# A hybrid decoder step on one core: new order of work in both token mixers, with sample numerators and decay logits cut into pieces between dense products

## The chip, the core and the metric

The kernel runs on one core of a Trainium2 chip. The metric is the device time of one execution in microseconds, lower is better. Five engines share the work: TensorE (matrix products, PE in the rows, its weight loads PEld), VectorE (DVE), ScalarE (ACT), GpSimd (POOL, idle here) and SyncE (SP), which issues the transfers.

## What is computed

Two layers, each of FFN, token mixer, FFN, around a residual stream of 576 tokens (8 sample sequences of 8 tokens, one prompt of 512) by 1024 features, in float32:

```python
for l in range(DEPTH):                     # DEPTH = 2
    x = x + 0.5 * swiglu(rmsnorm(x, norm_w[l, 0]), ...)
    h = rmsnorm(x, norm_w[l, 1])
    y = mlstm_mixer(h, ...) if l % 2 == 0 else gla_mixer(h, ...)
    x = x + y
    x = x + 0.5 * swiglu(rmsnorm(x, norm_w[l, 2]), ...)
```

The first mixer (mLSTM) projects to queries and keys (4 heads of 128 each), passes them through a causal convolution over 4 tokens and SiLU, projects values (4 heads of 256), an output gate and two scalar gates per head, and runs a stabilised matrix memory. Prompt tokens are done in chunks of 128, sample tokens against a stored state of 8 x 128 x 256 per head, which is updated and written back. The second mixer (gated linear attention) has no convolution, but a decay for every key feature; the attention inside a chunk is built from eight level products (distances 1, 2, 4, ... 64), and after each level queries, keys and decays are rescaled before the next. Outputs are the token results and all new states.

## The kernel before

Everything is laid out with features on partitions, 576 tokens along the free axis. Each dense weight block (128 x 1024) is loaded into `raw` (4 slots), ScalarE copies it to `w_hi` in the reduced format (L990) and VectorE subtracts to get `w_lo` (`split`, L1310); a dense product is then three passes, high by high, high by low, low by high (`split_product`, 288 columns each, L423; value tiles are 256 columns wide, L613). A pair is two such blocks; `lo_done` tells TensorE that a block's halves are there, `pe_done` that a pair is done, `psum_free` that VectorE has emptied its banks. The order on every engine is written out by hand; each engine takes its instructions in that order, and a wait holds up all that stands behind it.

Around the change:

- **Projection of queries and keys, first mixer** (`mlstm_qk`). Four pairs; pair 0 and 1 give queries, pair 2 and 3 keys. For each pair VectorE runs `split_next`, evacuates the pair into `conv_buf` (`before_conv`), and does three taps for each block (`taps`, L1472); ScalarE does the first tap and SiLU. The gate logits of all heads (`row_logits`, `row_sums`, `row_maxima`, 4 partitions wide) stand behind the taps.
- **Heads, first mixer** (`mlstm_mix`). Per head: five value tiles, two output-gate blocks in halves (`o_part`), and between them scores, transposed keys, updates of the state, the prompt numerator, the sample numerator (`sample_numerator`: 32 products of 8 columns in the trace and 4 of 64, L641 and L644, then the denominators), sums of squares (L675, L677) and sample state updates (L667).
- **Projection and heads, second mixer** (`gla_qk`, `gla_mix`). The decay logits (`decay_logits`, L530) are products with 16 rows. In the head loop level products of head h+2 (L504, L507) stand between the parts of head h. Before a level product TensorE waits on `lq_ready`, which VectorE raises at the end of `take_level` for the level before (L1769 to L1781). VectorE evacuates the sample numerator in `take_sample` (L1577), the prompt's in `take_prompt` (L1585), sample updates in `take_sample_updates` (L1595), the sums in `variance` (L1800, L1801).

The head loop of the second mixer on TensorE before:

```python
o_part(ph, h + 1, 0, 1)
sample_out(h, 4), level(h + 2, at + 1)
o_part(ph, h + 1, 1, 0)
sample_updates_of(h, 0, 4), level(h + 2, at + 2)
o_part(ph, h + 1, 1, 1)
```

and on VectorE, before and after the change:

```python
take_sample(1, h, 4), take_level(h + 2, at + 1)
take_sample_updates(1, h, 0, 4), take_level(h + 2, at + 2)
take_o(ph, h + 1, 1)
take_sample_updates(1, h, 1, 4), take_level(h + 2, at + 3)
```

## Time and profile before

| | |
|---|---|
| median of 3 runs | 2420.64 us (2414.5 to 2421.11) |
| profiled execution, its own time | 2422.03 us |
| its span, first to last instruction | 2420.2 us |
| TensorE busy | 2366.1 us (98%), 17380 products |
| VectorE busy | 1073.6 us (44%) |
| ScalarE busy | 665.7 us (28%) |
| mean granted clock of TensorE | 0.982 |
| transfers | 201.28 MB, mean 83 GB/s |

The chain of waits runs over TensorE for 94% of the span. The clock is given as a share of 2.4 GHz. Where busy time is told for a stretch, an instruction that reaches beyond it counts with its part inside. A product's own duration in the timeline contains its way through the array, so products overlap; their pace is read from the distance of their starts.

### The profile page before, as it was taken

How to read it: one execution, taken by the hardware profiler on the slowest of the kernel's cores; microseconds unless marked ns; L12 is line 12 of the kernel's file. 1: busy time of each engine (PE TensorE's matmuls, PEld its weight loads, DVE VectorE, ACT ScalarE, POOL GpSimd, SP SyncE). 2: the span in 40 equal slices, each digit the busy share in tenths (PEclk: the TensorE clock that was granted, in tenths of full speed). 3: DMA queues.
4: the chain of work that ended last, by engine and by line, in shares of the span. 5: the costliest groups of instructions: out<-in, count | busy, mean ns of one | idle time of the engine just before them, and what ended most of it. 6: DMA issues, size and time to landing. Idle time of an engine off the chain costs nothing.

```text
span 2420.2 us, 39582 instructions
## 1 busy us (share of the span) xinstructions
PE 2366.1 (98%) x17380; PEld 2332.7 (96%) x17380; DVE 1073.6 (44%) x1378; ACT 665.7 (28%) x801; POOL 0.2 (0%) x4
## 2 busy tenths in 40 slices
PE   7999999889999999999999999999999999999996
PEld 7999999889999999999999999999999899999996
DVE  5434324575445443334554333353764444334234
ACT  4212213443233321222332122234221333212122
POOL 0000000000000000000000000000000000000000
PEclk9999999999989999999999999999999999999998
DMA  4222222133222222222222222222122222222221
GB/s 169 87 87 70 86 87 70 60 106 104 87 77 92 87 87 70 87 87 66 91 87 84 73 87 87 65 91 88 50 76 73 86 76 87 87 87 74 83 74 52
DMA packets 71399, 201.28 MB, mean 83 GB/s; under 512 B 7140, under 2 KB 24804, under 8 KB 71296
## 3 DMA queue, kind: packets, MB, share of 16 engines
q1 hardware_dynamic: 71296, 199.79, 25.5%
q8 instruction: 78, 1.28, 0.2%
q14 instruction: 25, 0.20, 0.0%
HBM read 187.82 MB, written 11.95 MB: 83 GB/s over the span
## 4 chain that ended last, share of the span: by engine, by line
PE 94%; DVE 3%; ACT 1%; issue 1%; DMA 1%; SPq 0%; DVEq 0%; ACTq 0%
PE ps L423 82%; PE ps L613 4%; PE ps L504 1%; PE ps L641 1%; PE ps L667 1%; PE ps L475 1%; DVE scratch L1472 1%; PE ps L675 1%; PE ps L630 1%; PE ps L656 1%; DVE w_lo L1310 1%; PE ps L659 0%; DMA bc<-rows_all 0%; ACT w_hi L990 0%; DVE scratch L1339 0%
## 5 line engine op out<-in xcount | busy, mean ns | idle before, releaser
L423 PE MATMUL ps<-xn_hi,w_hi 128*128 128x288 f32 x3328 | 722.0, 299 | 23.1 <-DVE w_lo L1310 20.0
L423 PE MATMUL ps<-xn_hi,w_lo 128*128 128x288 f32 x3328 | 715.8, 297 | 0.0
L423 PE MATMUL ps<-xn_lo,w_hi 128*128 128x288 f32 x3328 | 715.7, 297 | 0.0
L423 PEld LDWEIGHTS ps<-xn_hi,w_hi 128*128 128x128 f32 x3328 | 540.2, 190 | 26.7 <-DVE w_lo L1310 12.1
L423 PEld LDWEIGHTS ps<-xn_lo,w_hi 128*128 128x128 f32 x3328 | 539.9, 190 | 0.0
L423 PEld LDWEIGHTS ps<-xn_hi,w_lo 128*128 128x128 f32 x3328 | 539.3, 190 | 0.0
L990 ACT ACTIVATE w_hi<-raw 128x1024 fp32r<-128x1024 f32 x336 | 335.4, 1046 | 360.7 <-PE ps L423 330.1
L1310 DVE TENSOR_TENSOR w_lo<-raw,w_hi 128x1024 fp32r<-128x1024 f32 x336 | 395.9, 1219 | 62.2 <-ACT w_hi L990 60.1
L423 PE MATMUL ps<-h_lo,w_hi 128*128 128x288 f32 x1664 | 358.5, 297 | 2.6 <-DVE h_hi L1610 2.6
L423 PE MATMUL ps<-h_hi,w_hi 128*128 128x288 f32 x1664 | 358.0, 297 | 0.0
L1348 DVE TENSOR_TENSOR scratch<-ps,rstd 128x576 f32<-128x576 f32 x88 | 66.6, 757 | 536.9 <-PE ps L423 533.9
L423 PE MATMUL ps<-h_hi,w_lo 128*128 128x288 f32 x1408 | 301.4, 296 | 0.0
L423 PEld LDWEIGHTS ps<-h_lo,w_hi 128*128 128x128 f32 x1664 | 269.5, 190 | 3.4 <-DVE h_hi L1610 3.4
L423 PEld LDWEIGHTS ps<-h_hi,w_hi 128*128 128x128 f32 x1664 | 269.4, 190 | 0.7 <-DVE h_lo L1357 0.7
L1022 ACT ACTIVATE scratch<-scratch 128x576 f32<-128x576 f32 x88 | 60.4, 687 | 723.2 <-DVE scratch L1348 723.1
L1379 DVE SCALAR_TENSOR_TENSOR x<-ps,x 128x1152 f32<-128x1152 f32 x56 | 76.0, 1357 | 353.9 <-PE ps L423 353.9
L423 PEld LDWEIGHTS ps<-h_hi,w_lo 128*128 128x128 f32 x1408 | 226.9, 189 | 0.0
L613 PE MATMUL ps<-w_hi,xn_hi 128*128 128x256 f32 x320 | 98.3, 307 | 3.8 <-DVE w_lo L1310 3.8
L1357 DVE TENSOR_TENSOR h_lo<-scratch,h_hi 128x576 fp32r<-128x576 f32 (+1 forms) x88 | 66.8, 759 | 73.8 <-ACT h_hi L1024 73.8
L613 PE MATMUL ps<-w_hi,xn_lo 128*128 128x256 f32 x320 | 94.8, 296 | 0.0
L613 PE MATMUL ps<-w_lo,xn_hi 128*128 128x256 f32 x320 | 94.6, 296 | 0.0
L1024 ACT ACTIVATE h_hi<-scratch 128x576 fp32r<-128x576 f32 (+1 forms) x88 | 60.4, 686 | 81.2 <-DVE scratch L1354 81.2
(209 smaller groups left out, 1507.8 us busy)
## 6 DMA issues: line engine op xcount, KB each, us to landing
raw<-in_w_gate SPq DMA_DIRECT2D x88, 512.0 KB, 3.7
raw<-in_w_up SPq DMA_DIRECT2D x88, 512.0 KB, 4.5
raw<-in_w_down SPq DMA_DIRECT2D x64, 512.0 KB, 3.9
raw<-in_w_mix SPq DMA_DIRECT2D x64, 512.0 KB, 4.1
raw<-in_w_down SPq DMA_DIRECT2D x32, 384.0 KB, 3.5
state_s<-in_state_c SPq DMA_DIRECT2D x4, 1024.0 KB, 8.1
out_c_s<-state_s SPq DMA_DIRECT2D x4, 1024.0 KB, 4.5
state_s<-in_state_g SPq DMA_DIRECT2D x4, 1024.0 KB, 7.6
```

The costliest lines, as they stand in the source:

```text
L423: ins = nc.tensor.matmul(o, a, b[:, c] if c is not None else b, start=first and j == 0, stop=last and j == 2)
L475: ins = nc.tensor.matmul(ps[:, j, HALF_TOK:HALF_TOK + 192], ones, T2(5)[:, a, 192 * j:192 * (j + 1)], start=a == 0, stop=a == 1)
L504: ins = nc.tensor.matmul(ps[:, bank, c * P:(c + 1) * P], left[:, ts], right[:, ts], start=True, stop=True)
L613: ins = nc.tensor.matmul(out, a[:, k, xs], b[:, 2 * half:2 * half + 2, ws], start=k == 0 and j == 0, stop=k == KT_X - 1 and j == 2)
L630: ins = nc.tensor.matmul(ps[:, 4 + c // 2, (c % 2) * DV:(c % 2 + 1) * DV], k_tok[:, c, :], v_tok[:, 1 + c, h * DV:(h + 1) * DV], start=Tru ...
L990: nc.scalar.activation(w_hi[:, slot, :], raw[:, slot, :], ACT.Copy).then_inc(hi_done, 1)
L1022: nc.scalar.activation(T(0), T(0), ACT.Silu).then_inc(silu_done, 1)
L1024: nc.scalar.activation(h_hi[:, bass.ds(m, 1), :].rearrange("p o t -> p (o t)"), T(2), ACT.Copy)\
L1310: V.tensor_tensor(w_lo[:, slot, :], raw[:, slot, :], w_hi[:, slot, :].bitcast(f32), ALU.subtract).then_inc(lo_done, 1)
L1348: V.tensor_tensor(cut2(T(0)), ps[:, b:b + 2, 0:HALF_TOK], cut2(rstd[:, :]), ALU.mult)\
L1357: V.tensor_tensor(h_lo[:, bass.ds(m, 1), :].rearrange("p o t -> p (o t)"), T(2), hh, ALU.subtract)\
L1379: ins = V.scalar_tensor_tensor(xs, ps[:, b:b + 4, 0:HALF_TOK], scale, xs, ALU.mult, ALU.add)
```

## The change

1. First mixer, projection: the queries and keys of one head form a pair (the weight blocks are laid out in that order). The split of the pair after next stands ahead of the convolution work on VectorE and ScalarE; `conv_buf` has four buffers in place of two; the tap results lie in `og` in three places; half of the taps are moved into the head stage. Rows for the broadcast are transferred ahead of one weight load.
2. First mixer, heads: TensorE, VectorE and ScalarE get a new order; gate columns come after the first value tile, sums of squares later, and for head 1 also updates and keys.
3. Sample numerators of both mixers run in pieces (`sample_piece`), each behind the products of one k of a dense block: eight pieces in a value tile, four in half a gate block.
4. Second mixer: decay logits are issued one head at a time inside the second block of a pair; the parts of head h move one place later on TensorE, relative to the level products. `gla_mix` of VectorE and ScalarE is as before.
5. Keys are signalled (`ktok_ready`) before the batch copies are made (`ktb_ready`).

```diff
-                load_mix(base + 2, 0, 10)
                 sp.wait_ge(rexp_done, 1)
                 for row, src in enumerate((T(6), T(7), T(3))):
                     sp.dma_start(io["rows"][row, :, :], src[0:N_HEADS, :]).then_inc(rows_out, 16)
-                load_mix(base + 3, 0, 18)
+                load_mix(base + 2, 0, 10)
                 sp.wait_ge(rows_out, 48)
-                sp.wait_ge(silu_qk, KT_X)
-                sp.wait_ge(tail_done, KT_X)
                 rows_load(0, bc_m, 0)
                 rows_load(1, bc_w, 0)
                 rows_load(2, bc_f, 0)
+                load_mix(base + 3, 0, 18)
+                sp.wait_ge(conv_ready, KT_X)
...
+            def sample_piece(mixer, h, bank, i, n):
+
+                a, per = 2 * i // n, 2 * DEC_BATCH // n
+                vs = slice(h * DV + a * P, h * DV + (a + 1) * P)
+                ds = slice(a * P, (a + 1) * P)
+                first = (i % (n // 2)) * per
+                for b in range(first, first + per):
+                    ts = slice(b * DEC_SEQ, (b + 1) * DEC_SEQ)
+                    nc.tensor.matmul(ps[:, bank, a * SAMPLE + b * DEC_SEQ:a * SAMPLE + (b + 1) * DEC_SEQ],
+                                     state_s[:, b, ds], qt[:, h, ts],
+                                     start=b == 0, stop=True, skip_group_check=True)
+                if first + per == DEC_BATCH:
+                    ins = nc.tensor.matmul(ps[:, bank, a * SAMPLE:(a + 1) * SAMPLE], v_tok[0:SAMPLE, 0, vs],
+                                           att(mixer, h)[0:SAMPLE, SEQ:TOK], start=False, stop=True,
+                                           skip_group_check=True)
+                    if a == 1 and mixer == 1:
+                        ins.then_inc(num_s_done, 1)
...
+                            if mixer == 1 and pp == 2 and blk == 1 and k in (0, 4):
+                                if k == 0:
+                                    pe.wait_ge(psum_free, base + 2)
+                                    pe.wait_ge(alow_ready, 1)
+                                decay_logits(k // 4, 4 + k // 2)
+                            if mixer == 1 and pp == 3 and blk == 1 and k in (0, 4):
+                                if k == 0:
+                                    pe.wait_ge(psum_free, base + 3)
+                                decay_logits(2 + k // 4, k // 2)
                         if blk == 0 and pp == 0:
                             early_gates(mixer, base)
-                        if mixer == 1 and blk == 0 and pp == 2:
-                            pe.wait_ge(psum_free, base + 2)
-                            pe.wait_ge(alow_ready, 1)
-                            decay_logits(0, 4)
-                            decay_logits(1, 6)
-                        if mixer == 1 and blk == 0 and pp == 3:
-                            pe.wait_ge(psum_free, base + 3)
-                            decay_logits(2, 0)
-                            decay_logits(3, 2)
...
                 for h in range(N_HEADS):
                     if h == 0:
                         rstd_columns(ph)
                     v_tile(ph, h, 0)
-                    v_tile(ph, h, 1)
-                    if h:
-                        sums_of(h - 1), scores(h)
+                    if h == 0:
+                        gate_columns()
+                    if h == 1:
+                        v_tile(ph, h, 1, sample_part(0))
+                        sample_den(0)
+                    else:
+                        v_tile(ph, h, 1)
+                    if h > 1:
+                        sums_of(h - 1)
+                    if h != 1:
+                        scores(h)
                     v_tile(ph, h, 2)
-                    if h:
+                    if h == 1:
+                        sums_of(0), scores(1)
+                    if h > 1:
                         sample_updates_of(h - 1, 0)
-                    else:
-                        gate_columns()
                     v_tile(ph, h, 3)
                     if h:
-                        sample_updates_of(h - 1, 1)
+                        sample_updates_of(h - 1, 0 if h == 1 else 1)
+                    v_tile(ph, h, 4)
+                    if h == 1:
+                        sample_updates_of(0, 1)
+                    if h != 1:
+                        keys_out(h)
+                    o_part(ph, h, 0, 0)
+                    if h == 1:
+                        keys_out(1)
                     else:
-                        scores(0)
-                    v_tile(ph, h, 4)
-                    keys_out(h)
-                    o_part(ph, h, 0, 0)
-                    updates_of(h)
+                        updates_of(h)
                     o_part(ph, h, 0, 1)
+                    if h == 1:
+                        updates_of(1)
                     o_part(ph, h, 1, 0)
                     prompt_out(h)
-                    o_part(ph, h, 1, 1)
-                    sample_out(h)
+                    if h:
+                        o_part(ph, h, 1, 1, sample_part(h))
+                        sample_den(h)
+                    else:
+                        o_part(ph, h, 1, 1)
...
                     updates_of(h), level(h + 2, at)
                     o_part(ph, h + 1, 0, 1)
-                    sample_out(h, 4), level(h + 2, at + 1)
-                    o_part(ph, h + 1, 1, 0)
-                    sample_updates_of(h, 0, 4), level(h + 2, at + 2)
+                    level(h + 2, at + 1)
+                    o_part(ph, h + 1, 1, 0, sample_part(h, 4))
+                    level(h + 2, at + 2)
                     o_part(ph, h + 1, 1, 1)
-                    sample_updates_of(h, 1, 4), level(h + 2, at + 3)
+                    sample_updates_of(h, 0, 4), level(h + 2, at + 3)
                     v_tile(ph, h + 1, 0)
-                    prompt_out(h), level(h + 2, at + 4)
+                    sample_updates_of(h, 1, 4), level(h + 2, at + 4)
                     v_tile(ph, h + 1, 1)
-                    sums_of(h, 4), level(h + 2, at + 5)
+                    prompt_out(h), level(h + 2, at + 5)
                     v_tile(ph, h + 1, 2)
+                    sums_of(h, 4)
                     if h == 0:
                         level(2, 7)
                         v_tile(ph, 1, 3)
...
                         v_tile(ph, 1, 4)
                         level(3, 1)
                     else:
+                        v_tile(ph, 2, 3)
                         keys_out(2)
-                        v_tile(ph, 2, 3)
...
+                R, base = slice(0, N_HEADS), ph["base"]
+                first_tap, silu = mlstm_conv(base)
+                split(ph, 0, 1)
+                gates_copy(0)
+                split(ph, 1, 0)
+                norm_root(ph["norm"])
+                first_tap(0)
+                first_tap(1)
+                act.wait_ge(rz_ready, 1)
+                own(nc.scalar.activation(T(5)[R], T(5)[R], ACT.Exp))
+                nc.scalar.activation(T(5)[R], T(5)[R], ACT.Ln, bias=1.0).then_inc(rz_exp, 1)
+                silu(0)
+                split(ph, 1, 1)
+                first_tap(2)
+                act.wait_ge(rexp_ready, 1)
+                nc.scalar.activation(T(5)[R], T(5)[R], ACT.Exp)
+                nc.scalar.activation(T(7)[R], T(7)[R], ACT.Exp)
+                nc.scalar.activation(T(3)[R], T(3)[R], ACT.Exp).then_inc(rexp_done, 1)
+                silu(1)
+                first_tap(3)
+                split(PHASES[j + 1], 0, 0)
+                silu(2)
+                first_tap(4)
+                silu(3)
+                first_tap(5)
+                split(PHASES[j + 1], 0, 1)
...
+                base = ph["base"]
+                split(ph, 0, 1)
+                dve.wait_ge(pe_done, base + 1)
+                norm_variance()
+                split(ph, 1, 0)
+                dve.wait_ge(rstd_ready, ph["norm"] + 1)
+                V.memset(conv_buf[:, :, CONV_P:CONV_P + TAIL], 0.0)
+                before_conv(0)
+                before_conv(1)
+                row_logits()
+                taps(0)
+                row_sums()
+                dve.wait_ge(pe_done, base + 2)
+                before_conv(2)
+                before_conv(3)
+                split(ph, 1, 1)
+                row_maxima()
+                taps(1)
+                dve.wait_ge(pe_done, base + 3)
+                before_conv(4)
+                before_conv(5)
+                split(PHASES[j + 1], 0, 0)
+                taps(2)
+                taps(3)
+                dve.wait_ge(pe_done, base + 4)
+                before_conv(6)
+                before_conv(7)
+                split(PHASES[j + 1], 0, 1)
...
+                take_rstd(0)
+                take_columns()
+                exponents(0)
+                taps(4)
+                take_v(ph, 0, 0)
+                take_scores(0)
+                taps(5)
+                take_v(ph, 0, 1)
+                taps(6)
+                take_v(ph, 0, 2)
+                take_keys(0)
+                taps(7)
+                split_at(2)
+                take_updates(0)
+                take_o(ph, 0, 0)
+                exponents(1)
+                for h in range(1, N_HEADS):
+                    take_o(ph, h - 1, 1)
+                    take_prompt(0, h - 1)
+                    if h == 1:
+                        split_at(3)
+                        take_v(ph, 1, 0)
+                    take_sample(0, h - 1, 7)
+                    denominator(h - 1)
+                    if h > 1:
+                        split_at(2 * h + 1)
                         take_v(ph, h, 0)
-                        variance(h - 1)
-                        take_scores(h)
-                        take_sample_updates(0, h - 1, 0, 4)
-                        take_v(ph, h, 1)
+                    variance(h - 1)
+                    take_scores(h)
+                    take_sample_updates(0, h - 1, 0, 4)
+                    take_v(ph, h, 1)
+                    if h > 1:
                         take_sample_updates(0, h - 1, 1, 6)
-                        normed(0, h - 1)
-                    else:
-                        take_rstd(0)
-                        take_v(ph, 0, 0)
-                        take_columns()
-                        exponents(0)
-                        take_v(ph, 0, 1)
-                        take_scores(0)
+                    normed(0, h - 1)
                     take_v(ph, h, 2)
-                    take_keys(h)
+                    if h == 1:
+                        take_sample_updates(0, 0, 1, 6)
+                    if h > 1:
+                        take_keys(h)
                     split_at(2 * h + 2)
-                    if h:
-                        low(0, h - 1)
+                    if h == 1:
+                        take_keys(1)
+                    low(0, h - 1)
                     take_updates(h)
                     take_o(ph, h, 0)
                     if h < 3:
...
-                                           bcast(sc[:, 1:], DK), ALU.mult, ALU.mult)
-                    sample_keys().then_inc(ktok_ready, 1)
+                                           bcast(sc[:, 1:], DK), ALU.mult, ALU.mult).then_inc(ktok_ready, 1)
+                    sample_keys().then_inc(ktb_ready, 1)
...
```

**Where instructions move, 1.** VectorE at the start of the first mixer's projection, from the taps of the first pair's second block (`scratch<-conv_buf`) over the row logits (4 partitions) to the next split (`w_lo`). Before:

```order
L1472 SCALAR_TENSOR_TENSOR scratch<-conv_buf,conv_w,scratch 128x600 [waits tap_done]
L1472 SCALAR_TENSOR_TENSOR scratch<-conv_buf,conv_w,scratch 128x600 [waits dve_chain] x2
L1408 TENSOR_TENSOR scratch<-scratch,rstd 4x576 [waits gates_copied]
L1409 TENSOR_TENSOR scratch<-scratch,rstd 4x576
L1410 TENSOR_SCALAR scratch<-scratch,gate_bias 4x576 [waits dve_chain]
L1411 TENSOR_SCALAR scratch<-scratch,gate_bias 4x576
L1398 SCALAR_TENSOR_TENSOR scratch<-scratch 4x576 [waits dve_chain]
L1310 TENSOR_TENSOR w_lo<-raw,w_hi 128x1024 [waits hi_done] x2
```

Now, from the split for the second pair (first row) on:

```order
L1369 TENSOR_TENSOR w_lo<-raw,w_hi 128x1024 [waits hi_done] x2
L1396 TENSOR_SCALAR scratch<-ps 128x576 [waits pe_done]
L1398 RECIPROCAL scratch<-scratch 128x576 [waits dve_chain]
L1369 TENSOR_TENSOR w_lo<-raw,w_hi 128x1024 [waits hi_done] x2
L1547 MEMSET conv_buf 128x4x3 [waits rstd_ready]
L1521 COPY conv_buf<-conv_in 128x8x3
L1522 TENSOR_TENSOR conv_buf<-ps,rstd 128x8x8
L1523 TENSOR_TENSOR conv_buf<-ps,rstd 128x224
```

The split of the third pair stood behind all six taps and the row logits of the first pair; it now stands directly behind the reciprocal, ahead of the evacuation.

**Where instructions move, 2.** TensorE in the head loop of the second mixer, head 0: the sample numerator (`ps<-qt,state_s` and `ps<-scratch,v_tok`) and the next level product (`ps<-qt,kt`). Before:

```order
L641 MATMUL ps<-qt,state_s 128x8 [waits states_ready,state_in]
L641 MATMUL ps<-qt,state_s 128x8 x7
L644 MATMUL ps<-scratch,v_tok 128x64
L641 MATMUL ps<-qt,state_s 128x8 x8
L644 MATMUL ps<-scratch,v_tok 128x64
L504 MATMUL ps<-qt,kt 128x128 [waits lq_ready0]
L504 MATMUL ps<-qt,kt 128x128 x3
L507 MATMUL ps<-qt,kt 64x64
L423 MATMUL ps<-xn_hi,w_hi 128x288 [waits psum_free,lo_done]
```

Now, from the last of the four pieces on, with the dense products of its k:

```order
L422 MATMUL ps<-xn_hi,w_hi 128x288 x2
L422 MATMUL ps<-xn_lo,w_hi 128x288 x2
L422 MATMUL ps<-xn_hi,w_lo 128x288 x2
L518 MATMUL ps<-qt,state_s 128x8 x4
L522 MATMUL ps<-scratch,v_tok 128x64
L503 MATMUL ps<-qt,kt 128x128 [waits lq_ready0]
L503 MATMUL ps<-qt,kt 128x128 x3
L506 MATMUL ps<-qt,kt 64x64
L422 MATMUL ps<-xn_hi,w_hi 128x288 x2
```

Before, 24 dense products followed the level product (the first shown). Now they are interleaved with the numerator, this level product has moved ahead of them, and the one behind the last piece is the next.

**Where instructions move, 3.** VectorE at the same place, which reads the same before and now but for line numbers: the end of one level, the gate block (`og<-ps`), the evacuation of the numerator (waits `num_s_done`), one whole level, and the state updates.

```order
L1873 TENSOR_TENSOR bc<-bc 128x288 [waits dve_chain]
L1613 TENSOR_TENSOR og<-ps,rstd 128x576 [waits mx_done]
L1651 TENSOR_TENSOR scratch<-ps,og 128x2x64 [waits num_s_done,og_done]
L1861 COPY_PREDICATED scratch<-level_mask,ps 64x64 [waits lvl_done0]
L1863 COPY_PREDICATED scratch<-level_mask,ps 128x512
L1868 TENSOR_TENSOR kt<-kt,bc 128x144x2
L1870 TENSOR_TENSOR qt<-qt,bc 128x144x2
L1873 TENSOR_TENSOR bc<-bc 128x144 [waits dve_chain]
L1669 SCALAR_TENSOR_TENSOR state_s<-state_s,scratch,ps 128x256 [waits us_half]
```

Nothing moved here. The last of the five rows of a level raises the semaphore for which TensorE waits ahead of the next level product.

## Rows read from the trace of the kernel before

**Rows 1.** Busy time and granted clock (after POOL's busy time) by stretch.

```profile
476.33:486.57 10.24, 4.90 (x20) 4.93 (x21) 6.40 (x14) 7.52 (x12) 0.00 (x0) 0.50 0.31 102
565.08:568.49 3.41, 3.41 (x19) 3.41 (x17) 0.05 (x1) 3.38 (x6) 0.00 (x0) 0.50 0.00 0
739.16:742.57 3.41, 3.01 (x12) 3.01 (x13) 1.91 (x5) 0.00 (x0) 0.00 (x0) 0.50 0.14 50
1674.41:1677.82 3.41, 3.41 (x16) 3.41 (x16) 0.00 (x0) 3.39 (x7) 0.00 (x0) 0.50 0.00 0
1906.51:1909.93 3.42, 3.42 (x16) 3.34 (x16) 0.00 (x0) 0.00 (x0) 0.00 (x0) 0.50 0.00 0
559.67:564.52 4.85, 4.85 (x42) 4.67 (x41) 0.76 (x1) 0.00 (x0) 0.00 (x0) 1.00 0.02 3
```

**Rows 2.** Timeline of TensorE (one row), then its list of waits: total, times, longest.

```profile
481.67 0.58 PE L423 MATMUL ps<-xn_hi,w_hi 128*128 128x288 f32 x1 [7.83 <-DVE w_lo L1310]
...
PE ps L613 <- DVE w_lo L1310: 3.8, 1, 3.8
PE ps L675 <- ACT scratch L1113: 3.0, 3, 1.3
PE ps L630 <- DVE k_tok_b L1497: 2.8, 2, 2.0
...
PE ps L423 <- DVE v_tok L1551: 1.9, 1, 1.9
```

**Rows 3.** Chain of waits in order of time: start, duration, what.

```profile
30.20 428.91 PE ps L423 x3216
...
481.67 15.22 PE ps L423 x96
...
1698.94 1.20 PE ps L570 x10
...
1706.04 3.40 PE ps L423 x24
...
1728.56 2.87 PE ps L613 x24
```

**Rows 4.** VectorE by stretch, first mixer: length, busy (instructions), clock, DMA.

```profile
461.10:465.64 4.54, 4.50 (x2) 1.00 0.00 0
466.41:468.33 1.92, 1.83 (x10) 1.00 0.00 0
468.33:473.36 5.03, 4.89 (x6) 1.00 0.00 0
473.36:476.65 3.29, 3.17 (x6) 0.95 0.00 0
480.30:482.66 2.36, 2.36 (x4) 0.50 0.09 14
489.53:493.70 4.17, 3.81 (x8) 1.00 0.00 0
503.87:509.40 5.53, 5.38 (x15) 1.00 0.01 3
545.48:549.58 4.10, 3.78 (x16) 1.00 0.61 197
```

**Rows 5.** VectorE by stretch, second mixer, the same columns.

```profile
1762.10:1762.39 0.29, 0.29 (x1) 0.50 0.00 0
1764.44:1766.34 1.90, 1.90 (x5) 0.50 0.00 0
1770.73:1774.07 3.34, 3.34 (x9) 1.00 0.00 0
1777.38:1780.44 3.06, 3.06 (x9) 1.00 0.14 48
1784.53:1787.15 2.62, 2.62 (x5) 1.00 1.01 339
1790.33:1792.75 2.42, 2.29 (x6) 1.00 0.07 20
```

240 lines of the change are left out of this document (110 added, 130 removed).

## Prediction

> **What bounds the kernel now.** I read the table of time by engine first: TensorE is busy 98% of the span, and no other engine half of it. So only two things can change the time: TensorE's idle time, and TensorE's pace while it works. For the pace I took the busy-time table over stretches, whose clock column shows 1.00 at 2.4 GHz and 0.50 at 1.2 GHz [rows 1]. The low time comes in stretches of 3.41 us or multiples of that. The first mixer has thirteen such units in seven stretches (44.4 us; TensorE works 37.7 of it, and 5.3 of the rest is in the first), the second eight in six stretches (27.3 us, all working); the first and last of each are shown. Two kinds of event stand ahead of them. Either TensorE had just waited (the stretch at 476.33), or it had just run a block of small products without a pause: 4.85 us of sample numerators end at 564.52, and the clock is low from 565.08, TensorE busy throughout [rows 1].
>
> The timeline and the list of waits of TensorE give those of the first mixer [rows 2]: 7.83 and 3.8 us for a weight's low half, 1.9 for value tiles, 0.8 for keys and 3.0 in three waits for squares, 17.3 in all. The second mixer has one, the longer of the two for keys (2.0 of 2.8 us). It brought no low stretch; the wait of 3.8 did.
>
> What a low stretch costs is read from the chain of waits [rows 3]: 3216 dense products took 428.91 us, 0.133 each; the 96 that begin at 481.67 should take 12.8 and took 15.22. TensorE was at 1.2 GHz for the first 4.9 us of them (to 486.57), so a low microsecond costs 0.49 and a unit of 3.41 costs 1.7. The low clock costs the first mixer 0.49 x 37.7 = 18.5 us now, the second 13.4.
>
> **First mixer, the projection of queries and keys.** Durations on VectorE are from [rows 4]: evacuating one pair 1.9 us, two tap chains 5.1 (one 2.6), row logits 3.3, row sums 4.2, row maxima 5.5, the two low halves of a pair 2.36, variance and reciprocal 4.5. I lay the new order end to end from 461.10, when the token sums are there. The reciprocal ends at 465.6 and the low halves of the third pair at 468.0, while TensorE needs them at 473.8: the 7.83 is gone. Evacuation to 469.9, logits 473.2, one tap chain 475.8, sums 480.0, evacuation 481.9, low halves of the fourth pair 484.2, needed at 486.6: the 3.8 is gone. Then maxima 489.7, taps 492.3, evacuation 494.1, first value weights 498.3, needed about 500.6, two tap chains 503.4, last evacuation 505.3. TensorE ends the projection at 499.4, spends 1.2 us on the columns of rstd and 2.9 on a value tile [rows 3], and stands at 503.5 before the gate columns, which want that last evacuation: a new wait of 1.75 us. VectorE then goes on without a pause to 535.5 (four tap chains are queued among value tiles, scores and keys); the prompt numerator of head 0 waits for it some 0.3 us. In head 1 the state updates now have one half block of 3.2 us as cover in place of two, against 4.1 us of states and weighted queries on VectorE: another 1.0. The row transfers start before 499 and end under the value tiles, so the 1.9 goes; keys are signalled before their batch copies, so the 0.8 goes; the squares get one or two value tiles as cover, so the 3.0 go. Waits: -17.3 + 3.05 = **-14.2 us**.
>
> The four sample numerators are cut into 8 or 4 pieces. A half block of 24 dense products behind small ones took 3.40 us instead of 3.20 [rows 3], so going back to dense work costs up to 0.2; zero is the other end; I take 0.1 for 16 more such changes: **+1.6** (0 to 3.2).
>
> Clock: the stretches behind the two long waits and half of those behind numerators should go. In four pieces, 0.8 us of dense work alternates with about 1 us of small work, and the denominators still follow the last piece, so it is no clean cure. Bounds are none left and all thirteen; I take six, 10.0 us: **-8.5**. First mixer: **-21.1 us**.
>
> **Second mixer, head loop.** This is the part that costs. TensorE's order changes and VectorE's does not. For heads 0 and 1 the level product of head h+2 used to follow the sample numerator; now the numerator runs in pieces up to the very next level product. That product needs the previous level's update, and VectorE has this update queued behind the evacuation of the numerator. The same happens four steps on: updates, prompt numerator and sums each stand directly ahead of a level product that needs an update queued behind their evacuation. Today a half block or value tile (3.2 or 2.9 us) lies between and hides it. Durations from [rows 5], plus 0.1 to 0.3 us for signals: evacuating the numerator 0.29 and a level 1.90, together 2.3 us; first state updates and a level 3.35, 3.5; second updates and a narrower level 3.05, 3.2; prompt and a level 2.6, 2.9; variance and a level 2.4, 2.5. Head 0: 14.4. Head 1 has the first four, with narrower levels: 11.5. Together **+25.9 us**, all on TensorE's path, because nothing else is queued there that could run meanwhile.
>
> Small terms: the decay logits are issued later in their pair, so the next pair waits some 0.4 for ScalarE to empty their banks; the keys of head 2 move behind a value tile, about 0.9 at the next one; the 2.0 shrinks by 1.2, since batch copies no longer stand ahead of the signal. Net +0.1. The pieces cost **+1.6** again.
>
> Clock: eight units now. Logits (two units) and numerators should keep about half of theirs, four. Nine new waits of 2.2 to 3.5 us lie between the 2.0 that left the clock alone and the 3.8 that lowered it, and state updates or sums run right before them, so I charge eleven units (bounds 0, and 18 for two each, as the wait of 7.83 had more than one). 15 units cost 25.1: **+11.7**. Second mixer: **+39.3 us**.
>
> **Sum.** -21.1 + 39.3 = +18.2. The profiled execution took 2422.0 us (span 2420.2), so 2440.2; the median of the runs is 1.4 lower: **2439 us**.
>
> **Rivals.** (a) *The clock holds, and it is faster.* The waits stay but none lowers the clock, and the spread products keep 2.4 GHz. First mixer -14.2 + 1.6 - 18.5 = -31.1, second 25.9 + 0.1 + 1.6 - 13.4 = +14.2: 2404 us. For it: the wait of 2.0. Against: nine waits are longer, and small products with no wait at all lowered the clock. It decides at ten units left in both mixers together (15.0 - 31.9 + 1.7 x 10 = 0.1); I forecast 21. Chance 0.08; 0.08 more for landing near ten. (b) *VectorE becomes the bound of the first mixer.* It is booked solid from 496 to 535.5; if the tap chains and splits run late by a few microseconds they delay gate columns, scores and the prompt numerator: about +10, 2449 us, chance 0.12. (c) *The next weights load behind a running dense product.* Then every piece hides its first load: 40 pieces times 0.12 (4.85 us for 42 products) is -4.8, and the +3.2 falls away: 2431 us, chance 0.08. Against: 0.20 us lost in the half block behind small products. The Trainium skill says this in "TensorE: Matmul & The Clock Gate", section "Step-by-step: what each phase is for": the next tile's weights load while the present matmul runs. The row differs by that 0.20. (d) *The second mixer's waits don't come*, because a wait I took as binding is met earlier: about 2395 us, chance 0.02, since the order of both engines is fixed in the code.
>
> The forecast has 0.62. The range 2423 to 2452 runs from (c) and a cheaper clock to (b). A measurement can tell 0.3%, 7 us: faster is (a) and (d), same the cases near ten units.
>
> **What would show it.** Right: no wait at the second and fourth projection pair of the first mixer; one of 1 to 3 us before the gate columns; nine waits of 2 to 3.5 us before level products of heads 2 and 3, released by VectorE; more than eight low units in the second mixer, fewer than ten in the first. Wrong: those waits missing or under 1 us, or no more low stretches there than now, or a first mixer shorter by under 15 us.

## The result, and the profile after

The changed kernel takes 2433.8 us (median of nine runs, 2424.3 to 2438.5), the kernel before 2421.1 beside it (nine runs, 2414.5 to 2422.2). The ratio is 1.0054, with a 95% interval of 1.0044 to 1.0065: slower by half a per cent, 12.7 us. The profiled execution took 2433.8 us, its span is 2432.0.

TensorE's token sums, twelve products in front of each stage, are the best milestones in the chain of waits. First the changed kernel (start, duration, what), then the kernel before:

```profile
458.59 1.97 PE ps L474 x12
766.63 1.95 PE ps L474 x12
...
1622.05 1.95 PE ps L474 x12
1997.50 1.95 PE ps L474 x12
```

```profile
459.11 1.96 PE ps L475 x12
795.54 1.95 PE ps L475 x12
...
1650.97 1.95 PE ps L475 x12
1985.97 1.95 PE ps L475 x12
```

The first mixer and its output projection went from 336.43 to 308.04 us (-28.4), what lies between them from 855.43 to 855.42, the second mixer with its output from 335.00 to 375.45 (+40.5). With -0.5 ahead of the first and +0.2 behind the second this is the whole difference of the spans, 11.8 us.

The busy-time table over the two mixers, up to their last output pair; columns are start:end, length, busy time (and instructions) of PE, PEld, DVE, ACT and POOL, granted clock, DMA share, GB/s. Before:

```profile
459.11:739.56 280.45, 261.90 (x1784) 246.17 (x1782) 153.63 (x305) 101.85 (x143) 0.00 (x0) 0.93 0.27 86
...
1650.97:1931.30 280.33, 277.01 (x1955) 261.05 (x1953) 152.11 (x282) 80.77 (x98) 0.00 (x0) 0.95 0.21 70
```

After, with four of its twelve low-clock stretches:

```profile
458.59:711.98 253.39, 250.07 (x1783) 235.18 (x1782) 153.47 (x305) 103.38 (x144) 0.00 (x0) 0.98 0.29 95
...
1622.05:1942.69 320.64, 291.83 (x1955) 273.42 (x1954) 151.02 (x282) 80.67 (x98) 0.00 (x0) 0.90 0.19 61
...
597.73:601.15 3.42, 3.42 (x18) 3.42 (x18) 1.98 (x3) 2.98 (x6) 0.00 (x0) 0.50 0.00 0
1730.96:1744.61 13.65, 11.41 (x50) 10.86 (x49) 2.08 (x6) 0.28 (x1) 0.00 (x0) 0.50 0.00 1
1812.88:1823.12 10.24, 8.13 (x35) 7.91 (x36) 1.95 (x6) 0.28 (x1) 0.00 (x0) 0.50 0.00 1
1874.32:1887.97 13.65, 13.65 (x55) 12.41 (x56) 2.54 (x6) 0.28 (x1) 0.00 (x0) 0.50 0.00 1
```

Length less PE's busy time is TensorE's idle time: 18.6 to 3.3 us in the first mixer (-15.2), 3.3 to 28.8 in the second (+25.5). The rest is the same work at another pace: 261.9 to 250.1 (-11.8) and 277.0 to 291.8 (+14.8). The clock column moves with it, 0.93 to 0.98 and 0.95 to 0.90. The first mixer has three low units left of thirteen (10.2 us in place of 44.4), the second nineteen in ten stretches in place of eight; TensorE works 58.5 us of those 64.8, against 27.3 before. The last of the ten stretches begins with the output projection, behind the end of the row, and 3.3 of the 58.5 us lie there. The other 55.2, less 27.3, are 27.9 us more at the low clock, and at the prediction's 0.49 that is 13.7 of the 14.8 that the busy column gained. In the first mixer the same working gives 12.1 for the 11.8 by which the column fell. What makes up the last 1.1 in the second mixer was not read apart.

The list of waits of TensorE after the change: what it waited for, us in total, times, the longest. It answers to [rows 2].

```profile
PE ps L503 <- DVE bc L1873: 25.0, 9, 3.4
PE ps L422 <- DVE w_lo L1369: 11.4, 1, 11.4
...
PE ps L633 <- DVE v_tok L1625: 1.6, 1, 1.6
PE ps L664 <- DVE kt L1760: 1.3, 2, 0.9
PE ps L653 <- DVE k_tok L1880: 0.9, 1, 0.9
PE ps L700 <- DVE conv_buf L1525: 0.8, 1, 0.8
```

The one wait left for a weight's low half is that at the start of the program. The 7.8 ahead of the third pair of the projection and the 3.8 ahead of the first value tile are gone, those for squares and keys of the first mixer too. In their place stand the 0.8 before the gate columns and 1.3 before the prompt numerators of heads 0 and 1. The new top line has nine waits, all in front of level products. This is the first, in the timeline from the level product before head 0's numerator to the one behind it (start, us, engine, line, operation, out<-in; in brackets the idle time before and what ended it):

```profile
1726.56 0.33 PE L506 MATMUL ps<-qt,kt 128*64 128x64 f32 x2
...
1736.79 0.69 PE L522 MATMUL ps<-scratch,v_tok 64*128 64x64 f32 x2
1737.59 0.29 DVE L1651 TENSOR_TENSOR scratch<-ps,og 128x128 f32<-128x128 f32 x1 [11.05 <-PE ps L522]
1737.79 0.21 DVE L1861 COPY_PREDICATED scratch<-level_mask,ps 64x64 f32<-64x64 uint8 x1
...
1737.92 0.71 DVE L1863 COPY_PREDICATED scratch<-level_mask,ps 128x512 f32<-128x512 uint8 x1
1738.53 0.44 DVE L1868 TENSOR_TENSOR kt<-kt,bc 128x288 f32<-128x288 f32 x1
1738.89 0.45 DVE L1870 TENSOR_TENSOR qt<-qt,bc 128x288 f32<-128x288 f32 x1
1739.26 0.40 DVE L1873 TENSOR_TENSOR bc<-bc 128x144 f32<-128x144 f32 x1
...
1739.72 2.08 PE L503 MATMUL ps<-qt,kt 128*128 128x128 f32 x8 [2.24 <-DVE bc L1873]
```

The level's products were there at 1726.9, and VectorE idle for 11.05 us, nearly all of it after them, but the next instruction in its queue was the evacuation of the numerator. Only when TensorE had closed the numerator did it go on, and TensorE stood for 2.24 us until the level's update was through. An engine with half its time free makes the busiest one wait, by the order of its queue alone.

### The profile page after: what moved, and what is told of

It reads as the page before. It is cut to its first block, busy times and chain, and to the rows that moved or that the text cites. A ratio compares the mean times of both kernels' runs of the same rounds, so it can differ in the third digit from the quotient of the medians.

```text
span 2432.0 us, 39599 instructions
## 1 busy us (share of the span) xinstructions
PE 2369.2 (97%) x17380; PEld 2334.4 (96%) x17380; DVE 1072.5 (44%) x1378; ACT 665.9 (27%) x801; POOL 0.2 (0%) x4
## 3 DMA queue, kind: packets, MB, share of 16 engines
q1 hardware_dynamic: 71296, 199.79, 25.5%
## 4 chain that ended last, share of the span: by engine, by line
PE 94%; DVE 5%; ACT 1%; issue 0%; DMA 0%; DVEq 0%; SPq 0%; ACTq 0%
PE ps L422 81%; PE ps L633 5%; PE ps L503 2%; PE ps L675 1%; PE ps L518 1%; PE ps L474 1%; PE ps L664 1%; DVE w_lo L1369 1%; PE ps L683 1%; PE ps L653 1%; PE ps L667 0%; DVE state_s L1669 0%; DVE og L1533 0%; DVE scratch L1398 0%; PE ps L522 0%
## 5 line engine op out<-in xcount | busy, mean ns | idle before, releaser
L422 PE MATMUL ps<-xn_hi,w_hi 128*128 128x288 f32 x3328 | 721.9, 299 | 11.8 <-DVE w_lo L1369 11.4
```

What stands on the lines that cost most here:

```text
L422: ins = nc.tensor.matmul(o, a, b[:, c] if c is not None else b, start=first and j == 0, stop=last and j == 2)
```

## The experiments

**Theory 1:** the nine waits are there because VectorE's order was left as it was when TensorE's was changed, and most of the low clock of the second mixer follows from them. **Rivals:** the pieces bring the low clock; or VectorE is short of time and the waits would only move. Nine edited kernels ran, two of them twice, in three groups; all numbers first. Each group had the kernel before beside it (2420.5, 2421.6 and 2420.5 us), and a ratio is to that of its own group. The last two columns are from token sums to token sums in the one profiled execution, which can lie off the median: that of half_order was the fastest of its six, that of vec_order the slowest of four, that of te_order_r the slowest of five (2400.9 us, the others 2385.8 to 2392.1).

| kernel | median us | ratio to before (95%) | profiled span | first mixer and output | second mixer and output |
|---|---|---|---|---|---|
| before | 2421.1 | 1 | 2420.2 | 336.4 | 335.0 |
| after | 2433.8 | 1.0054 (1.0044-1.0065) | 2432.0 | 308.0 | 375.5 |
| vec_order | 2385.9 | 0.9858 (0.9843-0.9873) | 2389.8 | 305.0 | 335.8 |
| te_order | 2384.5 | 0.9864 (0.9848-0.9881) | 2381.6 | 306.5 | 325.7 |
| mixer2_old | 2391.8 | 0.9880 (0.9862-0.9898) | 2391.5 | 308.1 | 335.2 |
| blocks1 | 2440.4 | 1.0086 (1.0071-1.0100) | 2438.6 | 316.8 | 373.0 |
| te_logits | 2387.7 | 0.9866 (0.9844-0.9887) | 2388.1 | 308.1 | 332.0 |
| te_blocks23 | 2389.0 | 0.9869 (0.9853-0.9885) | 2388.6 | 303.5 | 336.3 |
| vec_blocks | 2389.4 | 0.9871 (0.9856-0.9886) | 2385.0 | 308.1 | 329.8 |
| te_late_split | 2389.0 | 0.9884 (0.9864-0.9904) | 2386.3 | 311.3 | 327.2 |
| half_order | 2411.0 | 0.9962 (0.9949-0.9975) | 2402.8 | 308.1 | 347.1 |
| vec_order_r | 2390.0 | 0.9880 (0.9863-0.9896) | 2385.3 | 303.6 | 332.7 |
| te_order_r | 2387.4 | 0.9860 (0.9845-0.9874) | 2399.1 | 315.8 | 335.1 |

**VectorE's order moved (vec_order).** The edit, in VectorE's loop over heads 0 and 1:

```diff
-                    take_sample(1, h, 4), take_level(h + 2, at + 1)
-                    take_sample_updates(1, h, 0, 4), take_level(h + 2, at + 2)
+                    take_level(h + 2, at + 1)
+                    take_sample(1, h, 4), take_level(h + 2, at + 2)
                     take_o(ph, h + 1, 1)
-                    take_sample_updates(1, h, 1, 4), take_level(h + 2, at + 3)
+                    take_sample_updates(1, h, 0, 4), take_level(h + 2, at + 3)
                     split_at(V_AT[1][h + 1] + 1)
-                    take_prompt(1, h), take_level(h + 2, at + 4)
+                    take_sample_updates(1, h, 1, 4), take_level(h + 2, at + 4)
                     take_v(ph, h + 1, 0)
-                    variance(h, 4), take_level(h + 2, at + 5)
+                    take_prompt(1, h), take_level(h + 2, at + 5)
+                    variance(h, 4)
                     if h == 0:
-                        normed(1, 0), take_level(2, 7)
+                        take_level(2, 7), normed(1, 0)
```

> The changed kernel with VectorE's order in the second mixer's head loop (heads 0 and 1) moved the way TensorE's was moved: each level update now stands ahead of the evacuation that it used to follow, so five places shift by one. TensorE's order and the pieces stay. Theory 1 (the nine waits are there because VectorE's queue was left in the old order, and most low-clock stretches of the second mixer follow from them): the nine waits, 25.0 us, all go, the second mixer's low units fall from 19 to about 9, worth 1.7 us each, so 2433.8 - 25 - 17 = 2392 us (2386 to 2400). Rival 1 (the low clock comes from the numerators in pieces and not from the waits): the waits go, 19 units stay, 2409 us. Rival 2 (VectorE has no slack in this loop, so the wait only moves to the state updates and the prompt numerator): under 8 us gained, 2426 us or more.

Measured: 2385.9 us, 47.9 below the changed kernel and 1.4% below the kernel before. Theory 1 had said 2392 (2386 to 2400), so it lies 0.1 under the lower end, and far from both rivals. A level product of head 0's stretch without its wait, and the one in front of which TensorE still stands, by the timeline:

```profile
1742.94 1.16 PE L503 MATMUL ps<-qt,kt 128*128 128x128 f32 x8
...
1771.09 1.16 PE L503 MATMUL ps<-qt,kt 128*128 128x128 f32 x8 [0.68 <-DVE qt L1852]
```

Of the nine waits none is left; the one of 0.68 is another, for a diagonal. The second mixer has three low stretches; the third, at 1898.70, is one unit:

```profile
1728.03:1738.27 10.24, 10.24 (x45) 9.76 (x46) 1.32 (x4) 0.28 (x1) 0.00 (x0) 0.50 0.01 2
1833.84:1844.08 10.24, 10.24 (x39) 9.00 (x39) 2.55 (x6) 0.28 (x1) 0.00 (x0) 0.50 0.00 0
```

Seven units in place of nineteen, the pieces being the same. Its length with the output fell by 39.6 us: 24.3 is TensorE's idle time (28.8 to 4.5), the other 15.3 is pace. Both rivals fall: the pieces did not keep the nineteen units, and VectorE had room enough. That the pieces bring none is not shown. Eleven of the changed kernel's nineteen units begin within a numerator in pieces (at 1730.96, 1812.88 and 1874.32), the first four of them ahead of the first of the nine waits. At these places vec_order keeps six units; of the eight units elsewhere it keeps one.

That the low clock follows the waits doesn't rest on one profile of each kernel. Over all executions the mean granted clock was 0.979 to 0.986 in the changed kernel (nine), and 0.989 to 0.994 in this order (eight, with the repetition below).

**TensorE's order put back (te_order).** The other way to make the queues fit, with the numerators of heads 0 and 1 as blocks (`whole` issues the two parts of a numerator behind one another):

```diff
-                    level(h + 2, at + 1)
-                    o_part(ph, h + 1, 1, 0, sample_part(h, 4))
-                    level(h + 2, at + 2)
+                    whole(sample_part(h, 4)), level(h + 2, at + 1)
+                    o_part(ph, h + 1, 1, 0)
+                    sample_updates_of(h, 0, 4), level(h + 2, at + 2)
                     o_part(ph, h + 1, 1, 1)
-                    sample_updates_of(h, 0, 4), level(h + 2, at + 3)
+                    sample_updates_of(h, 1, 4), level(h + 2, at + 3)
                     v_tile(ph, h + 1, 0)
-                    sample_updates_of(h, 1, 4), level(h + 2, at + 4)
+                    prompt_out(h), level(h + 2, at + 4)
                     v_tile(ph, h + 1, 1)
-                    prompt_out(h), level(h + 2, at + 5)
+                    sums_of(h, 4), level(h + 2, at + 5)
                     v_tile(ph, h + 1, 2)
-                    sums_of(h, 4)
```

> The changed kernel with TensorE's order in the second mixer's head loop (heads 0 and 1) put back to the old one: the two sample numerators as unbroken blocks after the second half block, updates, prompt numerator and sums one place earlier. The rest of the change stays, also the numerators of heads 2 and 3 in pieces. Theory 1: the nine waits (25.0 us) go and the old wait for keys of about 1 to 2 us comes back; of the 14 low units inside the loop about 5 stay as in the kernel before, so 10 in the second mixer in place of 19: 2433.8 - 25 + 1 - 15 = 2395 us (2389 to 2401). Rival 1 (the small products' form sets the clock, not the waits): blocks bring at least as much low clock as pieces, 2410 us. If the pieces are worth something of themselves, this kernel is slower than the one with VectorE's order moved; if they cost, it is faster.

Measured: 2384.5 us, with no wait for a level's update left. I had set it at 2395 (2389 to 2401), and it fell below that range, since I expected ten low units in the second mixer; the profile shows two.

**The first mixer alone (mixer2_old).** As te_order, with the logits' edit shown further below and this:

```diff
-                updates_of(2)
-                v_tile(ph, 3, 1, sample_part(2, 7))
+                updates_of(2), whole(sample_part(2, 7))
+                v_tile(ph, 3, 1)
...
-                o_part(ph, 3, 1, 1, sample_part(3, 7))
+                whole(sample_part(3, 7))
+                o_part(ph, 3, 1, 1)
...
-                        v_tile(ph, 2, 3)
                         keys_out(2)
+                        v_tile(ph, 2, 3)
```

> The changed kernel with the second mixer's TensorE program put back as a whole: decay logits as two blocks behind the first block of a pair, all four sample numerators as blocks in the old places, keys of head 2 ahead of its value tile. Only the first mixer's part of the change is left, with the new order of query and key tiles. Theory 1 (the two mixers are independent, the first gives 27 us by the traces, the second takes 40): 2421.1 - 27.1 for the first mixer - 1.3 for the low stretch at its end - 0.5 at the start = 2392 us (2388 to 2397), and 8 low units in the second mixer as before. Rival (part of the first mixer's gain is a shift of the clock that comes back wherever the rest of the program is unchanged): 2400 us or more.

Measured: 2391.8 us, with nine low units in the second mixer. So the first mixer's part is worth 28.7 us by itself in the group's own comparison (before: 2420.5), and the two mixers can be added up. The early signal for keys stayed in, so the second mixer isn't the old one to the last instruction; its length is (335.2 against 335.0 us).

**The first mixer's numerators as blocks (blocks1).**

```diff
-                        v_tile(ph, h, 1, sample_part(0))
+                        v_tile(ph, h, 1)
+                        whole(sample_part(0))
                         sample_den(0)
...
-                        o_part(ph, h, 1, 1, sample_part(h))
+                        o_part(ph, h, 1, 1)
+                        whole(sample_part(h))
                         sample_den(h)
```

> The changed kernel with the four sample numerators of the first mixer as unbroken blocks again, each right behind the dense part that it was spread over and ahead of its denominators; nothing else altered. Theory A (the pieces keep TensorE's clock up): the low stretches behind the numerators come back, seven units before against one now, 6 x 1.7 = 10 us, less up to 2 us for the changes between small and dense products that go away: 2443 us (2438 to 2446). Theory B (the low clock went because the waits went, the pieces only cost): 2432 us or a little less, and no more than three low units in the first mixer.

Measured: 2440.4 us, its interval above that of the changed kernel: the pieces are worth some 7 us here, where I had said 9. Nine low units stand in its first mixer, seven of them at the four numerators. The medians carry this reading and the count of units does not: te_order_r below has its first mixer in pieces, and seven units beside its numerators all the same. The cost of the pieces themselves can be read where the clock is high. A half block with its numerator in pieces, in the chain of the changed kernel (head 2):

```profile
639.24 0.80 PE ps L422 x6
640.04 0.79 PE ps L518 x8
640.83 0.89 PE ps L422 x6
641.72 0.79 PE ps L518 x8
642.51 0.36 PE ps L522 x2
642.88 0.99 PE ps L422 x6
643.86 0.79 PE ps L518 x8
644.65 0.90 PE ps L422 x6
645.56 0.79 PE ps L518 x8
646.35 0.36 PE ps L522 x2
```

From 639.24 to 646.71 it is 7.47 us. The same work apart: the half block as blocks1 has it, and a numerator at the high clock, in te_order:

```profile
640.67 3.18 PE ps L422 x24
```

```profile
1724.81 1.68 PE ps L518 x16
1726.49 0.36 PE ps L522 x2
1726.85 1.88 PE ps L518 x16
1728.73 0.36 PE ps L522 x2
```

3.18 + 4.29 = 7.47 us as well. The dense quarters are 0.1 to 0.2 longer behind small products, 3.58 against 3.18 together, as I had charged them; the small ones are shorter by the same 0.4, 3.16 against 3.56 for 32 products.

**Logits, and the numerators of heads 2 and 3 (te_logits, te_blocks23).** Both start from te_order. The first puts the decay logits back into two blocks of 16 products:

```diff
-                            if mixer == 1 and pp == 2 and blk == 1 and k in (0, 4):
...
-                                decay_logits(k // 4, 4 + k // 2)
...
+                        if mixer == 1 and blk == 0 and pp == 2:
+                            pe.wait_ge(psum_free, base + 2)
+                            pe.wait_ge(alow_ready, 1)
+                            decay_logits(0, 4)
+                            decay_logits(1, 6)
```

and the same for the fourth pair. The second has the edit of mixer2_old above, and leaves the logits spread.

> The kernel with TensorE's old order in the head loop (2384.5 us), and the decay logits of the second mixer again as two blocks of 16 products, each behind the first block of its pair. Theory A (spreading the logits keeps the clock up): two low units come back, as they stand behind both logit blocks of the kernel before and of the run with the whole second mixer put back, 2 x 1.7 less about 0.2 for the changes between small and dense products: 2387.5 us (2386 to 2390). Theory B (spreading them is worth nothing): 2384.5 us within 1.

> The kernel with TensorE's old order in the head loop (2384.5 us), and the sample numerators of heads 2 and 3 of the second mixer as blocks in their old places, with the keys of head 2 ahead of its value tile. Together with the logits this makes up the difference to the run with the whole second mixer put back (2391.8 us, 7.3 us slower). Theory A (a numerator in one block lowers the clock): two to four low units come back near it, 2388 to 2391 us. Theory B (the four low units that the changed kernel has beside the pieces of head 2 come from the pieces): 2384 us or less.

Measured: 2387.7 and 2389.0 us, both where theory A had them. Two low units stand behind the logits again. But both intervals overlap with that of te_order, whose own repetition gave 2387.4, so a gain of 0 to 5 us each is all that can be said. The two together, mixer2_old, are 4.4 to 7.3 us above te_order's two medians, which speaks for a gain without proving it.

**Blocks with VectorE's order moved (vec_blocks).** As vec_order, with each numerator of heads 0 and 1 as a block behind the half block that it was spread over:

```diff
-                    o_part(ph, h + 1, 1, 0, sample_part(h, 4))
-                    level(h + 2, at + 2)
+                    o_part(ph, h + 1, 1, 0)
+                    whole(sample_part(h, 4)), level(h + 2, at + 2)
```

> The kernel with VectorE's order moved (2385.9 us), and the sample numerators of heads 0 and 1 of the second mixer as unbroken blocks right behind the half block that they were spread over. Its profile has three low units near each of these numerators though no wait of TensorE stands ahead of them. Theory A (in this place, with a level product on both sides and small products in between, pieces keep TensorE on small work for longer than a block does): the low units near the numerators fall from six to three or four, 2382 us. Theory B (pieces keep the clock up here as in the first mixer): four units more, 2392 us.

Measured: 2389.4 us, 3.5 above the one median of vec_order (2385.9) and 0.6 below the other (2390.0). Its second mixer has three low units, where the two profiles of vec_order have seven and five. Inconclusive: neither theory's number came.

**The third pair's low halves late (te_late_split).** As te_order, and in VectorE's program of the first projection:

```diff
                 norm_variance()
-                split(ph, 1, 0)
                 dve.wait_ge(rstd_ready, ph["norm"] + 1)
...
                 row_sums()
+                split(ph, 1, 0)
                 dve.wait_ge(pe_done, base + 2)
```

> The kernel with TensorE's old order in the head loop (2384.5 us), and in the first mixer's projection VectorE makes the low halves of the third pair's weights after row logits, one tap chain and row sums, not ahead of them. Laid end to end as in the prediction: the reciprocal ends at 465.1, evacuation 1.9, logits 3.3, taps 2.6, sums 4.2, low halves 2.4, so 479.5 against the 473 at which TensorE needs the first of them. Theory A (the wait that the change removed was the order of VectorE's work, and waits of this length lower the clock): a wait of 5 to 7 us at the third pair, with two or three low units behind it, of which TensorE works about half: 2384.5 + 6 + 4 = 2394 us (2390 to 2398). Theory B (something else had the wait, such as ScalarE's high halves or the weights' transfer): no such wait, 2385 us. Theory C (the wait comes, but the work behind it is short of nothing and catches up later): cannot be, TensorE being the bound, unless other waits fall by as much; under 3 us would show it.

The wait is there, as the timeline shows:

```profile
479.30 0.82 PE L422 MATMUL ps<-xn_hi,w_hi 128*128 128x288 f32 x2 [5.88 <-DVE w_lo L1373]
```

It shows that VectorE's place alone can bring such a wait. The time is 2389.0 us, under the 2390 to 2398 that I had set, and 4.5 and 1.6 above the two medians of te_order (2384.5, 2387.4). The intervals overlap, so the cost is not shown to be more than nothing, and it was less than the wait itself. The two profiles account for it as follows. The wait of 5.9 and two low units behind it (5.7 us with TensorE at work, 2.8 us) came. The 0.8 before the gate columns went, since all behind the wait came later, and so did the two low units that te_order has at 507.83 and 596.58 (3.3 us): 5.9 + 2.8 - 0.8 - 3.3 = 4.6, and the first mixer is 4.8 longer. Only the 0.8 is paid back by the later waits. The two units can be chance, for they come and go between executions of one program.

**Half of the waits (half_order).** The changed kernel, VectorE's order moved for head 1 only:

```diff
-                    take_updates(h), take_level(h + 2, at)
...
-                    variance(h, 4), take_level(h + 2, at + 5)
+                    if h == 0:
+                        take_updates(h), take_level(h + 2, at)
...
+                        variance(h, 4), take_level(h + 2, at + 5)
+                    else:
+                        take_updates(h), take_level(h + 2, at)
+                        take_o(ph, h + 1, 0)
+                        take_level(h + 2, at + 1)
+                        take_sample(1, h, 4), take_level(h + 2, at + 2)
...
+                        take_prompt(1, h), take_level(h + 2, at + 5)
+                        variance(h, 4)
```

> The changed kernel with VectorE's order moved in the second mixer's head loop for head 1 alone; head 0 keeps the old order, so that five of the nine waits (2.2, 3.4, 3.2, 2.8 and 2.3 us, 13.8 together) should stay and four (11.1) go. Theory 1 (each wait costs itself and some of the low clock behind it): it lies between the two kernels at 2385.9 and 2433.8. From the upper one: less 11.1 for the waits and up to 7 for the low stretches near them (14.3 us with TensorE at work, 0.49 each), 2416 to 2423. From the lower one: 13.8 and 0.49 x (27.1 - 10.2) = 8.3 for the low stretches that head 0 has in the changed kernel beyond those without waits, 2408. So 2413 us (2407 to 2421). Rival (a single place decides: one wait that puts all later work late, or one that shifts VectorE for the rest of the loop): close to one of the two ends, under 2400 or over 2426.

Measured: 2411.0 us, and 13.8 us in five waits. It lies in the middle, where the theory of separate waits puts it; no single place decides. The low clock is on theory 1's side only over the executions: their mean granted clock is 0.985 to 0.989, between the two ends. The profiled one, the fastest (2404.6), has six low units in the second mixer with its five waits, where vec_order has seven with none of them.

**Both repairs once more (vec_order_r, te_order_r),** with no edit.

> The kernel with VectorE's order moved once more, unchanged, since its profiled execution (span 2389.8 us) was 4 us above what its median would give and low stretches differ between executions. If only the place of the low stretches varies: median within 3 us of 2385.9, and a profile with the same waits of TensorE (0.7 us before a level product and no other in that loop) but other low stretches in the second mixer than three, three and one unit.

> The kernel with TensorE's old order in the head loop once more, unchanged, beside the one with VectorE's order moved. If the two are equally good ways to take the nine waits away, their medians lie within 3 us of each other, as at first (2384.5 and 2385.9). If pieces in the head loop are worth their six low units of the first profile, the one with VectorE's order moved is faster by up to 3; if they bring those units, slower by as much or more.

Measured: 2390.0 and 2387.4 us, within 3 of each other as at first. But 2390.0 is 4.1 above the first median of the same kernel, and I had allowed 3. Either order is 1.2 to 1.4% below the kernel before, and which is better was not settled. The profiles say why. Two of the four low stretches of te_order's mixers, the others again one unit each:

```profile
507.83:511.24 3.41, 3.41 (x19) 3.41 (x18) 3.30 (x10) 1.76 (x3) 0.00 (x0) 0.50 0.78 275
596.58:599.99 3.41, 3.41 (x17) 3.41 (x17) 2.09 (x3) 2.83 (x7) 0.00 (x0) 0.50 0.00 0
```

and two of the eight of te_order_r, the same program, both beside numerators in pieces:

```profile
591.75:601.99 10.24, 10.24 (x46) 10.10 (x47) 2.94 (x4) 2.94 (x6) 0.00 (x0) 0.50 0.00 0
...
697.57:704.39 6.82, 6.82 (x31) 6.68 (x30) 2.94 (x4) 3.54 (x7) 0.00 (x0) 0.50 0.00 0
```

Four units against sixteen, at 2381.6 and 2399.1 us of span, with the same instructions and the same waits behind the program's start. This pair prices the low clock with nothing else changed: TensorE works 20.5 us more of it in either mixer, and with their outputs the first is 9.2 us longer and the second 9.4. So a low microsecond costs 0.45 to 0.46, and a unit 1.6 us at most.

## Why the prediction was right, and by how much its steps were off

The sign, the place and the main term held: 2439 was forecast, 2433.8 measured, within the range. With their outputs the first mixer gave 28.4 us where 21.1 were forecast, and the second took 40.5 for 39.3.

- *Waits of the first mixer:* -14.2 forecast, -15.2 measured. All four kinds went. Of the new ones the gate columns took 0.77 in place of 1.75 (I had VectorE end the last evacuation at 505.3, it was through at 503.8), the two prompt numerators 0.38 and 0.89 for 0.3 and 1.0. The 4.2 us that I laid between 494.1 and the first value weights have no row behind them. In the trace VectorE waits 1.7 us there for ScalarE's high halves and is through with the low ones at 497.0, for 498.3.
- *Why the two long waits went:* the working went by VectorE's durations alone, and left out ScalarE, which has to copy a block's high half before VectorE can make the low one. In the kernel before, VectorE itself stood idle for that copy ahead of the third pair's low halves (3.69 us), and again ahead of the first value weights (2.84 us). The copy stood in ScalarE's queue behind convolution work and exponentials, and these wait for VectorE's row logits. So VectorE's split could not have been put ahead of the logits by itself, or each of the two engines would have waited for the other. The change moved both queues, and ScalarE now makes this copy at 460.58. The last row below also shows that the 3.8 stood ahead of the first value tile; there was no wait at the fourth pair, where the prediction has it. The kernel before:

```profile
479.23 1.98 ACT L990 ACTIVATE w_hi<-raw 128x1024 fp32r<-128x1024 f32 x2
480.30 2.36 DVE L1310 TENSOR_TENSOR w_lo<-raw,w_hi 128x1024 fp32r<-128x1024 f32 x2 [3.69 <-ACT w_hi L990]
...
514.64 0.58 PE L613 MATMUL ps<-w_hi,xn_hi 128*128 128x256 f32 x1 [3.77 <-DVE w_lo L1310]
```

- *Clock of the first mixer:* six units were to stay, three did in the profiled execution, and this is the largest error of the sum. Up to the output projection the first mixer came out at -27.1; the thirteenth unit, at the head of that projection, adds 1.3 (55.98 to 54.65 us). How many stay is no fixed number: ten of the profiles have this same first mixer, and show 3, 1, 0, 2, 8, 3, 3, 0, 3 and 3 units, with lengths of 303.5 to 315.8 us. So six was inside what the program does, and that three came was in part chance. The readings of the kernel before were slightly off: TensorE works 37.9 us of its 44.4 and not 37.7, and a low microsecond costs 0.45 and not 0.49.
- *Pieces:* +1.6 in each mixer forecast. The rows above show 0: the loss in the dense products was right, but I had left out what the small products gain. Rival (c) said that each piece hides its first load: it had this half right, and the +3.2 does fall away, but the 4.8 of gain it claimed is used up by the slower dense quarters. The Trainium skill, "TensorE: Matmul & The Clock Gate", section "Step-by-step: what each phase is for", says that the next tile's weights load while the present matmul runs. By this case's rows, going between small and dense products costs nothing on balance (7.47 us either way) and gains nothing.
- *Nine waits of the second mixer:* 2.3, 3.5, 3.2, 2.9, 2.5 forecast for head 0, 2.24, 3.41, 3.15, 2.76, 2.27 measured; 11.5 for head 1, 11.1 measured. 25.9 against 25.0: the sum of VectorE's durations for what is queued ahead, plus 0.1 to 0.3 for signals, gives such a wait to between one and two tenths. Experiments vec_order and te_order show its cause, from both sides.
- *Small terms of the second mixer:* +0.1 forecast, +0.5 measured (1.6 before a value tile and 0.9 for keys, against 2.0 before). The wait of 0.4 for the logits' banks didn't come.
- *Clock of the second mixer:* fifteen units forecast, nineteen measured, +11.7 against +14.8 us. Of the two units behind the logits one was to stay, none did. The mixer as a whole: +39.3 against +40.3, and with its output +40.5; the unit there cost 0.1 (54.67 to 54.81).
- *Rivals:* (a), the clock holds, is refuted by nineteen units; (b), VectorE bound in the first mixer, by the 2.0 us of waits there; (d) by the nine waits.

The sum missed by 6.4 us against the profiled execution (18.2 for 11.8). The first mixer with its output is 7.3 of it, 1.0 by its waits and the rest by its pace (clock and pieces); the second mixer takes 1.1 of this back. But the two profiles of te_order are 17.5 us apart by their low clock alone: for a single execution this term can't be forecast as closely as the waits, and that the count of 15 came near 19 was luck in part.

## What to carry to other kernels

When products are moved later in TensorE's program, move the evacuations in the other engine's program by the same step, or check for each of them that nothing between it and its consumer waits for later work: here one loop left in its old order turned a gain of 1.4% into a loss of 0.5%, with VectorE at 44% busy. Price such a wait by adding up the durations queued between the last signal and the consumer. Its cost in time need not be its length. In the second mixer here the waits cost about 1.6 times theirs by the profiles (39.6 us for 24.3), and 1.8 to 2.0 times by the medians (43.8 to 47.9 us), since low clock came with them. But the wait of 5.9 us that te_late_split put into the first mixer cost 1.6 to 4.5 by the medians, less than its length and not clear of the noise. So the factor is none to rely on in another place. And look at every engine ahead of the one that released the wait: ScalarE's queue had a share in the 7.8 us as well as VectorE's.

## What was not expected of the hardware

The low clock is not a property of the program. te_order and te_order_r, one program, had 13.7 and 54.6 us of it in their two mixers, and 17.5 us between their spans. The stretches shown lie by small products (numerators, levels, state updates, columns), so the places are mostly the program's and whether the clock falls there is not. For a single kernel it means that the medians of two measurements differed by 3 to 4 us (2384.5 and 2387.4; 2385.9 and 2390.0), and that a profile's count of low units should not be compared without a second one; the waits in it repeat to a tenth.

Small products suffer as much as dense ones. Eight numerator products took 0.96 us at the high clock (1724.93 in vec_order) and 1.71 at the low one, eight level products 1.05 to 1.16 and 2.07; a dense product takes 0.13 and 0.24 by the distance of starts (the changed kernel, from 1728.88 and from 1734.19):

```profile
1724.93 0.96 PE L518 MATMUL ps<-qt,state_s 128*128 128x8 f32 x8
...
1729.33 1.71 PE L518 MATMUL ps<-qt,state_s 128*128 128x8 f32 x8
```

The first lies 3 us ahead of the edge at 1728.03, the second 1.3 us behind it, TensorE working throughout: no wait stands ahead of that edge. What lets the clock fall in one execution and not in the next stays open.
